# Prompt queries by pairs of heads, their rotated part formed for all heads at once, and the fill-in work spread anew

## The reference, cut to what matters

```python
def mixer_layer(h, p, pos, ckv_past, krope_past, conv_past, ...):
    z = rmsnorm(h, ln_in) @ w_in
    c_q, c_kv, k_r, g_a, u_val, u_gate, g_c = jnp.split(z, [i1, i2, i3, i4, i5, i6], axis=-1)
    q = (rmsnorm(c_q, ln_q) @ w_q_b).reshape(b, t, N_HEADS_A, QK_NOPE + QK_ROPE)   # 64 plain + 32 rotated
    q_nope = q[..., :QK_NOPE]
    q_rope = rope(q[..., QK_NOPE:], pos)
    ...
    y_a = rmsnorm(o_a * jax.nn.silu(g_a), ln_out_a)
    u = u_val * jax.nn.sigmoid(u_gate)
    v = causal_dwconv(concat(past, u), conv_w, conv_b)
    v = jax.nn.silu(layernorm(v, ln_conv_g, ln_conv_b))
    y_c = rmsnorm(v * jax.nn.silu(g_c), ln_out_c)
    h = h + jnp.concatenate([y_a, y_c], axis=-1) @ w_out
    gate = jax.nn.sigmoid(rmsnorm(h, ln_pg) @ w_pg)
    h = h + gate * (p @ w_pe)

def rope(x, pos):        # x1, x2: the two halves of 16
    return jnp.concatenate([x1 * cos - x2 * sin, x1 * sin + x2 * cos], axis=-1)
```

## Time and profile before

| | |
|---|---|
| median of 3 runs | 793.55 us (793.33 to 793.84) |
| the profiled execution | 793.6 us |
| its span, first to last instruction | 791.8 us |
| TensorE (PE) busy | 768.0 us, 97% |
| TensorE weight loads (PEld) | 604.2 us, 76% |
| DVE (VectorE) busy | 566.2 us, 72% |
| ACT (ScalarE) busy | 417.6 us, 53% |
| POOL (GpSimd) busy | 65.1 us, 8% |

### The profile page before, as it was taken

The page is one execution under the profiler, slowest core; times in us unless marked ns, Lnnn a source line. Parts: engine busy times, 40 slices in busy tenths (PEclk is TensorE's granted clock), DMA queues, the critical chain, the costliest instruction groups (busy, mean ns, idle before and its releaser), DMA issues.

```text
span 791.8 us, 10529 instructions
## 1 busy us (share of the span) xinstructions
PE 768.0 (97%) x3767; PEld 604.2 (76%) x3767; DVE 566.2 (72%) x1094; ACT 417.6 (53%) x974; POOL 65.1 (8%) x114
## 2 busy tenths in 40 slices
PE   8999999999999999999999999999999999999995
PEld 7799877667767578888888988776676756888874
DVE  3459989887877685646463799897878686656477
ACT  3755655654455563353365484567444657323654
POOL 1400123200000310000000011222000000000000
PEclk9999999999999999999999999999999999999998
DMA  8722222100000154422181323111100004341203
GB/s 269 247 76 80 81 71 83 38 27 28 26 1 28 54 199 138 118 79 80 53 276 56 98 75 93 47 57 28 54 12 16 10 18 142 111 147 54 82 26 133
DMA packets 45833, 65.54 MB, mean 83 GB/s; under 512 B 12590, under 2 KB 24714, under 8 KB 45766
## 3 DMA queue, kind: packets, MB, share of 16 engines
q1 hardware_dynamic: 41946, 58.45, 23.1%
q0 software_dynamic: 3776, 6.40, 2.7%
q10 hardware_dynamic: 60, 0.02, 0.0%
HBM read 57.87 MB, written 7.18 MB: 82 GB/s over the span
## 4 chain that ended last, share of the span: by engine, by line
PE 84%; DVE 9%; ACT 5%; issue 2%; POOL 0%; ACTq 0%; DVEq 0%; POOLq 0%
PE acc L648 18%; PE acc L654 18%; PE acc L651 18%; PE acc L784 4%; PE sharedT L576 4%; PE sharedT L846 4%; PE sharedS L859 3%; PE sharedO L873 3%; PE sharedO L576 2%; PE sharedS L576 2%; DVE WLO L1432 1%; DVE VT L1505 1%; ACT WHI L1039 1%; PE sharedS L832 1%; PE sharedS L833 1%
## 5 line engine op out<-in xcount | busy, mean ns | idle before, releaser
L648 PE MATMUL acc<-WHI,XHI 128*128 128x512 f32 (+1 forms) x710 | 309.0, 435 | 1.1 <-ACT WHI L1039 0.5
L654 PE MATMUL acc<-WHI,XLO 128*128 128x512 f32 (+1 forms) x710 | 275.0, 387 | 0.0
L651 PE MATMUL acc<-WLO,XHI 128*128 128x512 f32 (+1 forms) x710 | 274.6, 387 | 0.3 <-DVE WLO L1432 0.3
L1505 DVE SCALAR_TENSOR_TENSOR VT<-UX,CWT,VT 128x640 f32<-128x640 f32 x240 | 211.9, 883 | 5.4
L648 PEld LDWEIGHTS acc<-WHI,XHI 128*128 128x128 f32 x710 | 133.8, 189 | 34.0 <-issue 8.8
L651 PEld LDWEIGHTS acc<-WLO,XHI 128*128 128x128 f32 x710 | 134.1, 189 | 30.8 <-issue 8.6
L1432 DVE SCALAR_TENSOR_TENSOR WLO<-WR,GT,WHI 128x512 fp32r<-128x512 f32 (+1 forms) x142 | 98.6, 736 | 76.8 <-ACT WHI L1039 76.4
L654 PEld LDWEIGHTS acc<-WHI,XLO 128*128 128x128 f32 x710 | 133.4, 188 | 26.0
L1039 ACT ACTIVATE WHI<-WR,GT 128x512 fp32r<-128x512 f32 (+1 forms) x142 | 93.6, 711 | 90.8 <-PE acc L654 90.6
L1242 ACT ACTIVATE SB<-SB,NBIAS 128x384 f32<-128x384 f32 (+1 forms) x80 | 45.7, 572 | 39.2 <-DVE NBIAS L1561 39.2
L873 PEld LDWEIGHTS sharedO<-V,PT 128*128 128x128 f32 x320 | 44.6, 191 | 16.1 <-issue 8.8
(11 more groups left out here) (197 smaller groups left out, 843.5 us busy)
## 6 DMA issues: line engine op xcount, KB each, us to landing
WR<-in_w_in_dram SPq DMA_DIRECT2D x32, 256.0 KB, 3.0
WR<-in_w_in_dram SPq DMA_DIRECT2D x16, 512.0 KB, 3.6
WR<-in_w_out_dram SPq DMA_DIRECT2D x16, 512.0 KB, 3.8
WR<-in_w_pg_dram SPq DMA_DIRECT2D x16, 512.0 KB, 3.5
H<-in_x_prompt_dram SPq DMA_DIRECT2D x16, 256.0 KB, 4.8
WR<-in_w_in_dram SPq DMA_DIRECT2D x8, 416.0 KB, 3.7
residual_spill<-H SPq DMA_DIRECT2D x5, 512.0 KB, 3.8
H<-residual_spill SPq DMA_DIRECT2D x10, 256.0 KB, 3.3
```

What stands on the lines that cost most here:

```text
L648: mm(out, hi, w_hi, start=(first and k == 0), stop=False)
L651: mm(out, hi, w_lo, start=False, stop=False)
L654: last = mm(out, lo, w_hi, start=False, stop=(final and k == 1))
L1505: ins = stt(out=out, in0=src, scalar=w, in1=out, op0=ALU.mult, op1=ALU.add)
```

## The change

- `load_wq` lays the query weights out by pairs of heads: for a pair, 64 columns of the first head's rotated part, 64 + 64 plain columns, 64 of the second head's rotated part. `queries(h)` takes the 128 plain columns of a pair at once, in sample step 7 (now in bank S) and in units 6, 14 and 22. For heads 0 and 1 DVE copies both halves out; for the later pairs ACT copies the first head (in two pieces) and DVE the second.
- `rotated_queries(half)` makes 16 of the 32 rotated columns for all heads, in sample steps 2 and 3 (bank O), from `WQR`, which POOL copies out of `WQ`. `rotate_queries` on DVE multiplies with cosine and sine (two operations each). In step 4 ACT issues eight DMAs that write the products to a buffer in DRAM, and POOL brings each head's 64 rows back into `QH` (now three slots). Heads 0, 1, 2 are fetched at the end of the sample steps, each of the others once the head three before it, whose slot it takes, has its last scores.
- The first tap of each channel group (k = 0, with the bias) goes from DVE to ACT (`first_tap`); 120 taps remain and are spread over units 0 to 27 (before 124 over 0 to 23).
- Filler: units get 1, 1, 2, 1 halves (before 1, 1, 2, 2), so block `gc` ends in unit 28, not 23. `turn_conv` is in units 29 to 31, `sample_heads` in unit 31. All `embed` calls, the norm of the convolution and the parts `high(20)`/`low(20)` stand behind the units.
- The splits of the parts of `gc` are now in units 2, 10 and 18; on DVE they follow the mask of the unit, and on ACT they stand at its head.
- In the units ACT's list is now: split, `probs(u + 1)`, copies of queries or keys, `probs_out(u)`, and last the copy and tanh of a completed tile (`block_out`). The same in sample steps 5 and 6.

```diff
-for _n, _m in [*enumerate([4, 4, 4, 4, 4, 4, 3, 3]), ("prep", 4), *((NB + u, (1, 1, 2, 2)[u % 4]) for u in range(UNITS))]:
+for _n, _m in [*enumerate([4, 4, 4, 4, 4, 4, 3, 3]), ("prep", 4), *((NB + u, (1, 1, 2, 1)[u % 4]) for u in range(UNITS))]:
...
-TAP_ORDER = [(c, k) for c in range(4) for k in range(TAPS)]
+TAP_ORDER = [(c, k) for c in range(4) for k in range(1, TAPS)]
...
-for _u, _m in enumerate((1, 3, 3, 2, 0, 2, 3, 2, 1, 2, 3, 1, 1, 3, 3, 2, 1, 2, 0, 2, 2, 2, 1, 2)):
+for _u, _m in enumerate((1, 1, 1, 3, 1, 1, 3, 2, 1, 1, 1, 3, 1, 1, 3, 2, 1, 1, 1, 3, 1, 1, 1, 1, 2, 1, 2, 2)):
...
-                    last = mm(bank((l, name))[:, :], WQ[:, k, h, :], CQT[:, k, 0:SEQ], start=(k == 0), stop=(k == 1))
+                    last = mm(bank((l, name))[:, :], WQ[:, k, h // 2, 64:192], CQT[:, k, 0:SEQ],
+                              start=(k == 0), stop=(k == 1))
+                fill_inc(last, (l, name))
+
+            def rotated_queries(half):
+                name = ("qr", half)
+                fill_wait(pe, (l, name))
+                pe.wait_ge(wqr_ready, 4 * (l + 1))
+                for k in range(2):
+                    w = WQR[:, k, half].rearrange("p g x e -> p (g x e)")
+                    last = mm(bank((l, name))[:, :], w, CQT[:, k, 0:SEQ], start=(k == 0), stop=(k == 1))
+                fill_inc(last, (l, name))
...
+                if s == 4:
+                    act.wait_ge(q_rotated, 2 * (l + 1))
+                    for half in range(2):
+                        copied_wait(act, (l, ("qr", half)))
+                    for h in range(HEADS):
+                        act.dma_start(q_spill[h].rearrange("x j n -> j x n"),
+                                      OTOK[NS * h:NS * (h + 1), 0:4, :]).then_inc(q_spilled, 16)
...
-            filler_out("prep")
+            probs_out(NB, 1)
             for u in range(UNITS):
                 h, i = divmod(u, 4)
+                split_high(NB + u)
+                if u < UNITS - 1:
+                    probs(NB + u + 1, P * ((i + 1) % 4 + 1))
                 for t in CONV_OUT.get(u, ()):
                     act.wait_ge(acc_filled[t], BLK[l, "cv"] + 1)
                     copy(VT[:, 512 * t:512 * (t + 1)], acc[t][:, :]).then_inc(acc_drained[t], 1)
...
+                if u:
+                    probs_out(NB + u, i + 1)
+                if u == 1:
+                    first_tap(3)
+                block_out(NB + u)
...
+            sample_heads_out()
+            norm_of_conv()
             head_out(HEADS - 1)
...
+            norm_of_conv_end()
+            for t in range(TILES):
+                normed(t)
+                if t == 2:
+                    low(first_i + 20)
```

More of the change, by code:

```diff
@@ L137, in shared_bank_plan @@
             order["O"].append((l, ("o", s)))
+            if s in (1, 2):
+                order["O"].append((l, ("qr", s - 1)))
             if s < NB - 2:
@@ L246, in build @@
         KRB = SB[:, 1, 0:32 * TILES].rearrange("p (t a e) -> p t a e", t=TILES, a=2)
+        COS8, SIN8 = QH[:, 0, :], OTOK[:, 4, :]
+        QROT = [OTOK[:, x, :] for x in range(4)]
         NBIAS = sb("NBIAS", [P, NB + UNITS])
@@ L317, in build @@
         rope_copied = sem("rope_copied")
+        rope8_in = sem("rope8_in")
+        q_second = sem("q_second")
+        q_rotated = sem("q_rotated")
+        q_spilled = sem("q_spilled")
+        q_rot_in = [sem(f"q_rot_in{slot}") for slot in range(3)]
         lnf_in = sem("lnf_in")
@@ L962, in tensor_layer @@
                 flip_probs(NB + u, P * (i + 1))
+            copied_wait(pe, (l, "p2"))
+            embed(0, 0)
+            values(UNITS - 1)
+            for t in range(1, TILES):
+                embed(0, t)
             embed(1, 0)
-            values(UNITS - 1)
             def turn_ya(t):
@@ L1174, in turned_u_out, with first_tap @@
                     drain_inc(out, (l, name))
+            def first_tap(c):
+                for part in range(2):
+                    copied_wait(act, (l, ("u", c, part)))
+                copied_wait(act, (l, "taps"))
+                copied_wait(act, (l, "gain"))
+                if l == 0:
+                    act.wait_ge(const_set, 9)
+                out = VTv[:, :, c, :].rearrange("p t (b j) -> p t b j", j=NS)
+                src = UX[:, c % 2, :, 0:NS].rearrange("p (t b) j -> p t b j", t=TILES)
+                av(out, src, ACT.Identity, scale=CWT[:, c, 0:1], bias=GT[:, l, G_CB + c:G_CB + c + 1]).then_inc(conv_begun, 1)
             def latent_out(t):
@@ L1819, in pool_layer, with halves_of_rotated @@
         def pool_layer(pool, l):
+            def halves_of_rotated():
+                pool.wait_ge(wq_in, 96 * (l + 1))
+                rot = WQ[:, :, :, :].rearrange("p k g (x c) -> p k g x c", c=64)[:, :, :, 0::3, :]
+                for k in range(2):
+                    for half in range(2):
+                        nc.gpsimd.tensor_copy(WQR[:, k, half], rot[:, k, :, :, 16 * half:16 * (half + 1)]).then_inc(wqr_ready, 1)
             if l:
@@ L1854, in pool_layer @@
                 pool.dma_start(SSUM[NS * s:NS * (s + 1), :], src[s], allow_slow_non_contiguous=True).then_inc(sums_in, 16)
+            for h in range(3, HEADS):
+                filled_wait(pool, (l, ("s", NB + 4 * (h - 3) + 3)))
+                rotated(h)
             filled_wait(pool, (l, "oa"))
```

217 lines of the change are left out of this document (131 added, 86 removed).

## The result

The changed kernel took **798.33 us** (median of 5 runs, 797.53 to 798.66) against 793.55 (793.12 to 793.84) for the kernel before beside it: a ratio of 1.0058, 95% interval 1.0046 to 1.0070. It is 0.6% slower, clearly more than the 0.2% that the prediction took as the least to be told from no change, where 790.7 was forecast, and it lies above the range of 780.5 to 796.5.

The account below looks back on a forecast made before the run. PE was taken as the bound, busy 768.0 of 791.8 us. Per layer, matmuls -3.44, sample steps +0.8, units' waits +1.1 and behind them +0.1 give -1.44, -2.9 for two: 790.7 us, range 780.5 to 796.5.

Parts of the forecast that it names:

- Queries on PE: Prompt and rotated queries: 12 matmuls a layer instead of 16, -3.4 us; sample queries, scores and keys keep their number.
- So I take 3: Sample step 4: eight DMA issues on ACT take 3 us, 2.7 covered, so +0.4 a layer (0 to 1.2).
- Rotated queries wait in bank O: +0.2 twice: Sample steps: rotated queries wait for the sample's values to be copied out of bank O, +0.2 us twice a layer.
- Step 7: Sample step 7: PE waits for ACT's copy before the pair's queries in bank S, +0.85; DVE's two query copies, +0.25.
- Units 0 to 22: together 1.9: Long stalls go; waits left at units 11 and 19 (0.5 each), paired queries (0.2 each of three), value rows (0.3).
- Units 23 to 31: some 7: Late gates delay masks and the next scores; PE waits 6.7 us up to values(31), some 7 with ACT's exponentials.
- Behind the units: After values(31): DVE's 15 us of work fits PE's about 17 before `oa0`; +0.1 us a layer (0 to 1.5).
- A: Gates fit after all: units wait 3 us a layel instead of 9, 778.7; chance 0.28 with halfway cases.
- B: Units 22 to 28: late gates also delay exponentials, flips and PT, +3 us a layer, 796.7; chance 0.12.
- C: PE has room, so waits fill half (794.1) or all (797.6) of the removed matmuls' 6.9 us; chance 0.15 plus 0.03.
- The reading of the weight loads: Weight loads fill 76% of the span, so PE has a quarter of room, which speaks for C and its 797.6.
- Wrong I am: Signs: gates under 2 us behind flips, waits of units 23 to 31 over 8 us, `oa0` waiting over 1 us.

Follow-up runs that it names:

- e1: Changed kernel with two DVE taps moved from ahead of the sample queries' copies to sample steps 3 and 5: 796.92 us.
- e2: Changed kernel with the eight DMAs that write the rotated products issued by POOL instead of ACT: 794.71 us.
- e11: e5 with ACT copying finished tiles ahead of PT again in sample steps 5 and 6, as in the kernel before: 786.8 us.
- e8: e5 with the tap ahead of mask(12) and mask(20), in units 10 and 18, moved to idle places: 783.04 us.
- e3: Changed kernel with a completed tile's gate one unit later in DVE's list, behind a mask: 790.39 us.
- e4: Changed kernel with a completed tile's copy and tanh ahead of the exponential and PT in ACT's unit list: 789.31 us.
- e12: e5 with the first pair's queries in bank T, the taps ahead of mask(12) and mask(20) moved, and head 0 copied by ACT: 780.23 us.
- e7: Kernel before the change with one of two prompt-query matmuls left out for heads 1, 3, 5 and 7 (queries incomplete): 788.82 us.
- e10: e5 with the pairs' prompt queries of units 6, 14 and 22 issued twice: 794.77 us.
- e5: Changed kernel with the changes of e1, e2 and e4 together: 783.83 us.

## Why the prediction was wrong

The forecast of 790.7 and the 798.3 measured are 7.6 us apart. By the table above and the runs:

1. **"The sum, for one layer" has no term ahead of step 0.** *Queries on PE* says that sample queries keep their number, which is true for PE; what the new layout does to their copies on DVE was not costed. It is +1.04 and +0.77, 1.8 of the 7.6, of which up to 0.5 may be scatter. e1 took 1.4 of it away.
2. **"So I take 3"** for the eight DMA issues was the wrong size. They took 5.1. I went by rows of issues at the start (0.28 and 0.47), and the upper bound of 3.8 came from these too. ACT's six there also stand in a row (0.73 to 2.96 us, the last five 0.28 to 0.32 each), but they load 1 to 4 KB; of ACT writing 128 KB from 16 partitions there was no row. Its first issue took 0.31 and the last six 0.71 each. Whether the number in a row, the size or the direction makes the price was not tested. The cover was 3.4 (5.1 less the 1.7 lost) rather than 2.7, as issuing began 0.9 before ACT's last copy of the cache had ended (143.14 and 144.00 in layer 0). The term was +0.4 and measured +1.7, 2.7 of the 7.6 for both layers. e2 shows it.
3. **"Rotated queries wait in bank O: +0.2 twice"** measured +0.34 twice; **"Step 7"** 0 and measured +0.3. The wait for bank S is 0.85 by distances, as forecast, and step 6's wait is gone, -1.1, also as forecast (e11); what failed is the two copies on DVE, 0.69 each instead of 0.6, behind which the units' first scores wait 0.67. Together 1.2 for both layers.
4. **"Units 0 to 22: together 1.9"** measured 3.9: units 11 and 19 lose 0.91 each instead of 0.5 (a wait for the mask and one for the copy of the keys), units 2 and 3, with value rows and keys, 0.87 instead of 0.3, and 0.1 to 0.2 in several others. Less the 0.4 by which the waits before were taken too small, and the 0.3 that point 5 came out better, it is 1.3 a layer, about the 1.1 by which the units' row of the table is off. e8 shows the part of units 11 and 19 (0.55 each); for units 2 and 3 and the small ones no run was made, so there the rows give the place and the cause stays open.
5. **"Units 23 to 31: some 7"** was right: 6.7, unit by unit nearly as laid out (0.8, 1.1, 1.2, 0.5, 1.3, 0.1, 1.2, 0.5 against 0.95, 1.12, 0.84, 0.50, 1.32, 0.11, 1.01, 0.89), with the first opening 2.9 us behind its flips. e3 and e4 confirm the chain. "Behind the units" was right too: `oa0` starts without a wait.

**The rivals.** A (gates fit) is refuted by the 6.7. That its 778.7 is near the 780.2 of e12 is chance: e12 gets there by another order and by cures elsewhere. The step that B names, the late mask holding up the exponential and PT, is there in the rows (237.08 and 237.48), but it was in the layout already and added nothing to it: the waits from unit 23 on stayed below B's 8 us. Its condition "over 10.4 us of waits" was met (10.6), by the waits of point 4. C holds in part in the kernel before (e7: 70% of the matmuls' price comes back), but e10 shows that it is not so in the changed kernel, where added matmuls cost all they take in units 6, 14 and 22. Of the units that lost their queries there, 10 and 18 pass in 3.01 and 3.02 us, which is their work, and 2 and 26 wait 0.4 and 0.5. The reading of the weight loads gave 797.6, and with the idle column scaled, which was my own step, 797.9, almost what came; yet it gave it because PE would have room, and e10 says it has none, and 780.2 was reached with nearly the same loads (601.5 us against 602.5). A number can be right by the wrong path.

**The signs.** None of the three signs of "Wrong I am" came: the gate ended 2.4 us behind the flips, the waits from unit 23 on were 6.7, and `oa0` started without one. All three look at stretches that were laid out in detail, and the misses lay outside them.

The step that failed most is the term for the DMA issues (2.7), then the units 0 to 22 (2.2) and the copies not costed (1.8). All have the same sign: they are costs of the new parts outside the stretch that I had laid out in detail, and against a gain of 2.9 any two of them turn the result.

## What to carry to other kernels

Price what a new layout does to every reader of it, also where the number of matmuls stays the same: the copies of the sample queries cost 1.8 here. In a list that runs in order, work that nobody waits for soon (a gate) should not stand ahead of work on which the next step hangs (a mask), or what it waits for should be produced early; moving either brought more than the whole change was forecast to bring. Which order is right depends on who waits: in sample steps 5 and 6 PT ahead of the tiles was the better one, by 1.1 a layer, with the same operations. Take the price of a DMA issue from issues of the same kind and number, and put them on an engine that is not on the path in that step. And give signs of being wrong for the stretches that were priced in a line as well.

## What the runs showed of the hardware

- Eight DMAs of 128 KB (16 partitions x 4 rows of 2 KB) to DRAM in a row held ACT for 5.1 us: 0.31 and 0.45 for the first two, 0.71 each for the other six. They held POOL for 4.08, 0.51 each. Loads of 1 to 4 KB, also in a row, took ACT 0.28 to 0.32 each.
- A DVE operation on 64 partitions took as long as one on 128 with the same columns (0.42 and 0.42 for 256 columns, above), and a copy over 64 x 512 took 0.69, as much as the gate over 128 x 512.
- In a unit where the weight loads fill 3.07 of 4.96 us, two added fp32 matmuls over 512 columns made it 1.71 us longer, their whole price (e5, e10).
